# A hybrid attention / gated-delta-net layer on one core: the filler of the scan is spread over its opening, and the last level of its block inverse works on a quarter of each block

## The reference, cut to what matters

```
decay = exp(where(tril_incl, g[:, None] - g[None, :], -inf))
lmat  = where(tril_strict, (k_beta @ k.T) * decay, 0)
t_inv = inverse(eye + lmat)                    # per chunk and head
u, w  = t_inv @ v_beta, t_inv @ (k_beta * exp(g))
a     = where(tril_incl, (q @ k.T) * decay, 0)
v_new = u - w @ state
o     = (q * exp(g)) @ state + a @ v_new
state = state * exp(g_last) + (k * exp(g_last - g)).T @ v_new
```

## Time and profile before

| | us |
|---|---|
| median of 3 runs (2967.61 to 2977.02) | 2967.79 |
| the profiled execution | 2968.09 |
| its span | 2966.3 |
| PE busy in the span | 2681.6 (90%) |
| DVE busy | 1400.3 (47%) |
| ACT busy | 1040.5 (35%) |
| POOL busy | 606.5 (20%) |

### The profile page before, as it was taken

The page is one execution under the profiler, slowest core; times in us unless marked ns, Lnnn a source line. Parts: engine busy times, 40 slices in busy tenths (PEclk is TensorE's granted clock), DMA queues, the critical chain, the costliest instruction groups (busy, mean ns, idle before and its releaser), DMA issues. The chain is left out here.

```text
span 2966.3 us, 46114 instructions
## 1 busy us (share of the span) xinstructions
PE 2681.6 (90%) x18134; PEld 2525.5 (85%) x18134; DVE 1400.3 (47%) x2320; ACT 1040.5 (35%) x1801; POOL 606.5 (20%) x489
## 2 busy tenths in 40 slices
PE   7999999589898999828999869989999999999999
PEld 3898999578888888726777758889999999999999
DVE  3565331157666766447888833352222242222222
ACT  4312332233343333136778733322222222222211
POOL 1001222434333433143323221210111000111100
PEclk9999999779897999858999979999999999999999
DMA  5324664334343433140000044332222233222232
GB/s 202 144 80 131 220 220 153 101 91 111 100 151 80 122 85 86 59 163 14 9 17 16 12 181 166 116 99 71 78 78 71 78 114 94 71 78 72 69 96 70
DMA packets 194779, 294.22 MB, mean 99 GB/s; under 512 B 82704, under 2 KB 121648, under 8 KB 192816
## 3 DMA queue, kind: packets, MB, share of 16 engines
q1 hardware_dynamic: 191728, 276.15, 29.6%
q10 hardware_dynamic: 2880, 15.73, 1.5%
HBM read 228.28 MB, written 63.52 MB: 98 GB/s over the span
## 5 line engine op out<-in xcount | busy, mean ns | idle before, releaser
L277 PE MATMUL f_ps<-mf_h_hi,mf_w_hi 128*128 128x320 f32 x1408 | 435.1, 309 | 1.4 <-PEq L1982 1.4
L277 PE MATMUL f_ps<-mf_h_hi,mf_w_lo 128*128 128x320 f32 x1408 | 435.1, 309 | 0.0
L277 PE MATMUL f_ps<-mf_h_lo,mf_w_hi 128*128 128x320 f32 x1408 | 435.1, 309 | 0.0
L2415 DVE TENSOR_TENSOR mf_w_lo<-mf_w_raw,mf_w_hi 128x1024 fp32r<-128x1024 f32 (+1 forms) x135 | 188.8, 1399 | 431.6 <-ACT mf_w_hi L2267 431.4
L277 PE MATMUL proj_ps<-h_hi,w_hi 128*128 128x320 f32 x896 | 282.7, 316 | 6.0 <-DVE w_lo L575 5.6
L277 PE MATMUL proj_ps<-h_hi,w_lo 128*128 128x320 f32 x896 | 278.0, 310 | 0.0
L277 PE MATMUL proj_ps<-h_lo,w_hi 128*128 128x320 f32 x896 | 278.0, 310 | 0.0
L277 PEld LDWEIGHTS f_ps<-mf_h_hi,mf_w_hi 128*128 128x128 f32 x1408 | 264.4, 188 | 1.6 <-issue 1.6
L277 PEld LDWEIGHTS f_ps<-mf_h_lo,mf_w_hi 128*128 128x128 f32 x1408 | 264.4, 188 | 0.0
L277 PEld LDWEIGHTS f_ps<-mf_h_hi,mf_w_lo 128*128 128x128 f32 x1408 | 264.4, 188 | 0.0
L2341 POOL TENSOR_TENSOR f_ff_lo<-f_ff_f,f_ff_hi 128x640 f32 (+1 forms) x44 | 69.3, 1576 | 783.1 <-ACT f_ff_hi L2267 783.1
(11 more groups left out here) (323 smaller groups left out, 6425.2 us busy)
## 6 DMA issues: line engine op xcount, KB each, us to landing
mf_w_raw<-w_up_dram SPq DMA_DIRECT2D x88, 512.0 KB, 3.5
w_ada_raw<-w_ada_dram SPq DMA_DIRECT2D x16, 1024.0 KB, 5.2
mf_w_raw<-w_mix_dram SPq DMA_DIRECT2D x32, 512.0 KB, 5.0
w_raw<-w_in_dram SPq DMA_DIRECT2D x28, 512.0 KB, 5.1
mf_w_raw<-w_down_dram SPq DMA_DIRECT2D x32, 448.0 KB, 3.3
delta_t<-delta_tile ACTq DMA_DIRECT2D x10, 1024.0 KB, 6.7
fill_raw<-w_in_dram SPq DMA_DIRECT2D x20, 512.0 KB, 4.2
kq_t<-delta_t SPq DMA_DIRECT2D x20, 512.0 KB, 4.3
```

The lines of the kernel that those rows point to most:

```text
L277: ins = nc.tensor.matmul(out, w(k), a(k), start=(first and n == 0 and q == 0), stop=(last and n == len(ks) - 1 and q == 2))
L2415: nc.vector.tensor_tensor(wlo[:, slot, 0:nk], raw[:, slot, 0:nk], whi[:, slot, 0:nk].bitcast(F32), ALU.subtract).then_inc(E[half]["lo"], 1)
```

## The change

It has two parts and what they need.

- **The table of the filler.** 6 matmuls per slot in bodies -3 and -2, 12 in body -1 (312 in the opening, before 52), 3 per slot in bodies 0 to 4 until the first ten tiles are done (in slot 3 of body 4) and from body 7 on, none in bodies 5 and 6.
- **The last level** (64 to 128) works only on the 64x64 blocks that it changes: its matmuls have 64 rows of weights and 64 moving columns where they had 128 and 128, DVE copies 64x256 without a mask, ACT copies two pieces of 64x256 instead of one of 128x1024.
- The weight buffers and their semaphores are shared between `in_projection` and `delta_scan`, so the first two filler tiles are loaded, and the first split, before the scan begins; room for it comes from reusing other buffers in `ada_and_norm`, where the first two loads of `w_in` now also wait for `cols_done`.
- SP's first issues in the scan are in another order, `x_base` is zeroed by DVE instead of POOL, and SP waits for that only before `inverse_in`.
- The second half of the tokens is reloaded in eight pieces of 640 KB over bodies 5 and 6.

```
-            for s in range(SLOTS):
-                plan(u, s, 4 if -1 <= u < NT - 1 or u >= NT else 0)
...
+        RELOAD = 5
+
+        def quota(u):
+            if u < 0:
+                return 12 if u == -1 else 6
+            return 3 if u < RELOAD or u >= RELOAD + 2 else 0
...
+                n = min(quota(u), 3 * KT - i % (3 * KT))
+                pieces[u, s] = []
+                if n and t < (FILL_TILES if u < RELOAD else NF):
+                    pieces[u, s] = [(t, i // (3 * KT), i % (3 * KT), i % (3 * KT) + n)]
+                    at[0] += n
...
+            def reload(u, i):
+                if u in (RELOAD, RELOAD + 1):
+                    n = 4 * (u - RELOAD) + i
+                    ks = slice(2 * (n // 2), 2 * (n // 2) + 2)
+                    if n == 0:
+                        sp.wait_ge(e["fill_ps"], 2 * FILL_TILES)
+                    sp.dma_start((h_hi, h_lo)[n % 2][:, ks].bitcast(F32), io["h_late"][n % 2][:, ks]).then_inc(e["h2_in"], 16)
...
-                            sp.dma_start(h_hi[:].bitcast(F32), io["h_late"][0]).then_inc(e["h2_in"], 16)
-                            sp.dma_start(h_lo[:].bitcast(F32), io["h_late"][1]).then_inc(e["h2_in"], 16)
...
-            nc.gpsimd.tensor_scalar(XB[:].rearrange("p t h i -> p (t h) i"), keep["ident"][:].unsqueeze(1).to_broadcast([P, 2 * NH, P]), 0.0, None, ALU.mult).then_inc(e["xb_zero"], 1)
...
+                            if lv < LV[-1]:
+                                nc.scalar.activation(XX[:, c].rearrange("p t h i -> p t (h i)"), BC[c][:], ACT.Copy).then_inc(e["x_ready"], 1)
+                            else:
+                                p, q = quarters(u)
+                                nc.scalar.activation(XX[q, c, 0, :, p], bankB(c)[q, :, 0:HD], ACT.Copy)
+                                nc.scalar.activation(XX[p, c, 1, :, q], bankC(c)[p, :, 0:HD], ACT.Copy).then_inc(e["x_ready"], 1)
...
+                                nc.vector.tensor_copy(Y[q, c, :, p], bank(a)[q, :, 0:HD]).then_inc(e["a_out"], 1)
...
+                                    last = mm(bank(a)[:, m, 0:HD], NI[p, u % 2, c, m], XX[p, c, 0, m, p])
...
+                                    mm(bankB(c)[:, m, 0:HD], XX[q, c, 1, m], Y[q, c, m, p])
+                                    last = mm(bankC(c)[:, m, 0:HD], Y[q, c, m], XX[q, c, 1, m, q])
```

More of the change, by code:

```diff
@@ L68, in ada_and_norm @@
         c_raw = sb("c_raw", [P, KT, 2])
[L69 to L73, removed]
+        rows = keep["w_raw"][0:2].rearrange("p t k n -> p (t k n)")
         hf = sb("h_f32", [P, HR, 3 * P])
+        bg_raw = hf[:, HR - 1, 0:KT * 32].rearrange("p (k n) -> p k n", k=KT)
+        bg_hi, bg_lo = (keep["w_lo"][:, p, 0:2].rearrange("p k n -> p (k n)").rearrange("p (k n) -> p k n", k=KT) for p in range(2))
+        bg_t = lambda b: x[0:32, TAPS[b][0], 0:span(b)[1] - span(b)[0]]
         sq = hf[:].rearrange("p r n -> p (r n)")[:, 0:D]
@@ L118, in _ @@
             sp.dma_start(bg_raw[:], io["w_bg"]).then_inc(bg_in, 16)
+            sp.wait_ge(cols_done, 1)
             for p in range(2):
@@ L225, in _ @@
                 for j in range(*TAPS[b]):
-                    last = nc.tensor.transpose(col_ps[:, 32 * j:32 * j + 32], bg_t[:, j * P:(j + 1) * P], keep["ident"][0:32, 0:32])
+                    last = nc.tensor.transpose(col_ps[:, 32 * j:32 * j + 32], bg_t(b)[:, (j - TAPS[b][0]) * P:(j - TAPS[b][0] + 1) * P], keep["ident"][0:32, 0:32])
             last.then_inc(bg_cols, 1)
@@ L799, in delta_scan @@
         o_stored = [sem(f"o_stored{i}") for i in range(2)]
-        fw_in = [sem(f"fill_in{i}") for i in range(2)]
+        fw_in = keep["w_in_sems"]
         f_stored = [sem(f"fill_stored{i}") for i in range(2)]
@@ L937, in _ @@
                     sp.dma_start(S[half(h), 1, d, :, h], io["state_in"][d, half(h)]).then_inc(e["state_in"], 16)
-            sp.wait_ge(e["xb_zero"], 1)
             for u in UNITS:
-                if has(u + 3):
-                    if u < 0:
-                        load_kq(u + 3)
+                if has(u + 3) and u >= -1:
                     load_rows(u + 3)
+                reload(u, 0)
                 for s in range(0, 3):
@@ L956, in _ @@
                     inverse_out(u + 1)
+                    if u == -1:
+                        sp.wait_ge(e["xb_zero"], 1)
                     inverse_in(u + 1)
+                reload(u, 1)
                 if u == 4:
@@ L970, in _ @@
                     blocks_out(u + 2)
+                reload(u, 2)
                 if has(u - 1):
@@ L976, in _ @@
                     blocks_in(u + 2)
+                reload(u, 3)
             sp.wait_ge(e["kept"], 64)
@@ L1201, in body @@
                     fill(u, 3 * len(LV) + 2 + c)
-            split_lo(0)
+            nc.vector.tensor_scalar(XB[:].rearrange("p t h i -> p (t h) i"), keep["ident"][:].unsqueeze(1).to_broadcast([P, 2 * NH, P]), 0.0, None, ALU.mult).then_inc(e["xb_zero"], 1)
             for u in UNITS:
+                if u == -2:
+                    dve.wait_ge(e["zeroed"], 4)
+                    dve.wait_ge(e["masks_in"], 32)
                 body(u)
@@ L2553, in build @@
         }
+        keep["w_in_sems"] = [ctx.enter_context(nc.semaphore(f"w_in{p}")) for p in range(2)]
         keep["first_sem"] = ctx.enter_context(nc.semaphore("first_sem"))
@@ L2563, in build @@
                 keep["c_act"] = c1.enter_context(nc.sbuf_tensor("c_silu", [P, KT, 2], F32))
-                keep["w_raw"] = c1.enter_context(nc.sbuf_tensor("w_raw", [P, 2, KT, P], F32))
-                keep["w_in_sems"] = [c1.enter_context(nc.semaphore(f"w_in{p}")) for p in range(2)]
                 keep["b_ada"] = c1.enter_context(nc.sbuf_tensor("b_ada_sb", [P, 48], F32))
@@ L2572, in build @@
                 keep["offdiag"] = sb2("offdiag_sb", [P, P])
[L2573 removed]
+                keep["levels"] = sb2("levels_sb", [P, LEVELS - 5, 2, P])
                 delta_scan(nc, io, keep, tab, h_hi[0], h_lo[0])
@@ L2589, in constants @@
     tri = np.stack([tri, tri.T], 1)
-    levels = np.zeros((P, LEVELS - 4, 2, P), np.float32)
-    for lv in range(4, LEVELS):
+    levels = np.zeros((P, LEVELS - 5, 2, P), np.float32)
+    for lv in range(4, LEVELS - 1):
         s = 2 ** lv
```

86 lines of the change are left out of this document (40 added, 46 removed).

## The result

The changed kernel takes 3015.64 us (median of 4 runs, 3006.06 to 3020.24) and the kernel before 2967.70 (4 runs on the same chip): ratio 1.0163, 95% interval 1.0146 to 1.018. It is 48 us slower; the forecast was 2962. The profiled execution took 3013.73 us with a span of 3011.8, 45.5 more than before.

The account below looks back on a forecast made before the run. It took a ring of SP, DVE and ACT (30.2 us a period), with PE beside it, as the bound; +1.7 - 3 - 3 + 5 - 3 - 2.5 - 1.3 = -6.1 took 2968.1 to 2962, range 2950 to 2974.

Parts of the forecast that it names:

- The ring: Scan bodies: SP, DVE and ACT hand work round in a closed 30.2 us period, with PE's 28.8 us beside it.
- PE is the bound: Rival: PE bounds the scan, so all 260 fillers taken from the bodies come off: 2927 us, chance 0.08.
- Last level on a quarter: Last inverse level: narrower matmuls keep their spacing of about 110 ns, smaller copies lie beside the ring: 0 us.
- Waits and the clock: Full bodies: longer PE idles drop the clock in about half, filler splits enter the ring: net +5 us.
- The -3 for SP's fewer loads: Scan bodies: 10 fewer filler loads and stores fall on SP in the ring: -3 us (0 to -8).
- the clock falls in every body: Rival: at the level-5 wait of 1.6 us and more, each full body loses clock: 2989 us, chance 0.14.
- State store, reload: Body 4's final-state wait, then the reload in eight pieces with the unfilled bodies: -3 and -2.5 us.
- Filler in the opening: Opening: 312 fillers mostly hidden under the DMA and DVE chain; unit 1's `inverse_out` at 629.5 for 627.79: +1.7 us.
- The warm unit: Unit 0: PE arrives at 2.4 GHz after a dense opening, the period after takes 30 and not 33.0: -3 us.
- The tail: After the last `inverse_out`, bound by PE and DVE: one filler less in 7 slots, shorter last-level copies: -1.3 us.

Follow-up runs that it names:

- e9: The changed kernel with the last level's matmuls back at 128 rows and 128 moving columns, the copies behind them left small: 2976.16 us.
- e12: e2 plus two cancelling matmuls (plus and minus the identity times h) in slot 5 of each filled body, right ahead of the wait for `attn_t`: 2965.94 us.
- e13: e2 with the last four of the reload's eight pieces issued by the middle of body 6, not by its end: 2969.80 us.
- e1: The kernel before with only the last inverse level on a quarter, its own filler table kept: 2996.32 us, ratio 1.0109.
- e2: The changed kernel with the last level whole again, its new filler table kept: 2977.79 us, ratio 1.0037.
- e4: The changed kernel with one matmul that computes nothing added to every filler piece from body 0 on: 3006.29 us.
- e16: e15 with the last level on a quarter put on top: 2961.90 us, ratio 0.9975.
- e3: The changed kernel with four filler matmuls per slot from body 7, so none are left for bodies 17 to 19: 3008.25 us.
- e15: The kernel before with early reload pieces, idle work in unfilled slots, cancelling pairs in slots 3 and 5, and SP's final-state wait and stores moved behind `blocks_in`: 2941.17 us.

## Why the prediction was wrong, point by point

- **The ring held.** Periods at a clock of 1.00 are 29.6 and 29.9 us in the changed kernel and 29.3 to 30.5 in the kernel before; with the whole level and three fillers the shortest are 28.6 to 28.7 (e9, e12, e13), so fewer fillers gain a part of a microsecond and not the 1.9 us of PE's work. The rival "PE is the bound" is out. One reading of the ring was wrong: DVE did not sit idle for the 2.9 us until `blocks_in` landed, but 0.52 us. That is all the room there was, so an engine that comes more than half a microsecond late is in the ring.
- **The step that failed: "Last level on a quarter", taken as 0.** Its PE part was right: at full clock the new matmuls start 0.67 us / 6 = 112 ns apart, predicted 105 to 110:

```profile
1273.23 0.27 PE L1220 MATMUL banks_bc<-x_inv,y_res 64*128 64x64 f32 x1
1273.90 0.27 PE L1220 MATMUL banks_bc<-x_inv,y_res 64*128 64x64 f32 x1
```

  By the Trainium skill ("TensorE: Matmul & The Clock Gate", LDWEIGHTS (loading the stationary operand)) a weight load's time goes by its columns and not by its rows. The trace agrees: at full clock a load of 128 columns is shown with 0.19 us for 64 rows (at 1273.20) as for 128 rows (at 1009.63 in the kernel before). But I asked only how long the matmuls take at full clock. With the narrow ones in the last level a fallen clock stays down for longer, and the term is 30 us (e1), or 39 in the changed kernel (e9), and not 0.
- **"Waits and the clock", +5.** The waits were forecast right in kind, but the price hung on a fall of 13.6 us that gives part back. With the whole level a fall behind the wait of 1.38 us for `attn_t` lasts 3.4 us, and bodies 11 to 18 together cost nothing (245.3 us in e2, 246.1 before); with the quarter falls last up to 20 and cost 5 us of a period. The -3 for SP's fewer loads can't be told apart in these 0.8 us. The rival "the clock falls in every body", with 0.14 of the chances, had the kind of loss right and not its place or size: it named level 5 and waits of 1.6 us, where six of the eight falls from unit 8 on stand behind last-level waits (1.38 in five of them), it had no part for the narrow level, and its 2989 is 27 us short.
- **"State store, reload", -3 and -2.5.** Body 4's period went from 41.0 to 39.5 at a mean clock of 0.59; in e2 it is 34.2. The two reload periods took 16.5 us more (36.0 and 40.5 for 30.5 and 29.5) and the one behind 3.9; the 10.3 us that the kernel before pays above 30.3 at its own reload did not come back, since falls filled that place. With the whole level they did: e2 is 7.6 us late at unit 1 and 9.1 at unit 11, so all bodies between, with the state store and both reloads, come to +1.5 there. I priced the pieces on the queue and missed that PE waits for the last one at the first slot of body 7 and starts it cold (e13: 8 us).
- **"Filler in the opening", +1.7.** Unit 0's `inverse_out` is at 603.93, unit 1's at 635.07 (629.5 forecast): +7.3. The rows of SP and PE in the changed kernel:

```profile
586.60 4.75 SPq L881 DMA_DIRECT2D diag<-n_t  x8
603.93 0.49 SPq L889 DMA_DIRECT2D diag_inv<-diag_inverse_pair  x1
```
```profile
619.91 1.00 PE L1220 MATMUL bank_A<-x_base,n_t_eye 128*128 128x128 f32 x8
```

  `blocks_out` left at 586.60 (583 forecast), and PE came at 619.91 (617). All profiles with this opening have unit 0 at 603.9 to 607.3, all without it at 595.6 to 599.0. The warm unit behind it gave 2.3 of the 3 forecast, in this profile; in the others with this opening that period took 30.3 to 33.3 us. No run has the opening alone, but the profile of e2 says where the table's own loss lies: it is 7.6 us late at unit 1, 8.3 at unit 19 and 8.2 at the end.
- **The tail, -1.3**, was +1.4: there too PE was at 1.2 GHz for a part. With the quarter this stretch took 54.1 us, 54.8 in e1, 54.4 in e4 and e16 and 62.3 in e3, which has no filler left there; with whole matmuls it took 48.6 to 52.7.

## What to carry to other kernels

Before thinning an engine's work because "it isn't the bound", ask what it idles for afterwards: here PE's idles of 1.38 us in front of a dependency were mostly followed by a fall of the clock. With whole matmuls behind them the falls were short and cost nothing in these bodies; with narrow ones they cost 20 us over eight. A smaller matmul that takes the same issue slot (112 ns here) saved nothing and went with longer falls, so leave it whole unless its slot gets shorter. Look for the ring first, and put single waits (a state store, the last piece of a reload) where neither the ring nor the head of a body stands behind them: that was worth 11 and 6 to 8 us here. And read a loss unit by unit before giving it to one part of a change: a stretch in which only one of two kernels reloads hides as much as it shows.

## What the runs showed of the hardware that I had not expected

- Over all 18 profiles, units 0 to 19, waits of 1.03 to 1.12 us for `attn_t` in front of the last level had a fall beginning within 2.6 us behind them in 12 of 58 cases (none of 6 before the change, 1 of 7 in e12), those of 1.36 to 1.42 us in 50 of 68 (5 of 7 in the changed kernel from unit 8 on, 8 of 9 in e2). It is no sharp line: at level 5 a wait of 1.04 us at 1048.20 in e12 had a fall behind it, and one of 1.81 us at 715.57 in e15 had none.
- How long a fall lasts went with the shape of the last level's matmuls, although PE is busy in nearly all of it: behind waits of 1.36 to 1.42 us always 3.4 us with 128x128 ones and the thin filler, up to 13.7 with half the rows, half the columns or both. What else decides it is open: whole levels too had falls of 10 to 17 us in the kernel before, behind waits at level 5 above all.
- Two matmuls per body that compute nothing made a kernel 12 us faster (e12 against e2), of which the profiles place 4.3 us between units 8 and 19.
